# Summing the squares of a block norm on GpSimd before two ones-matmuls, in place of eight ones-matmuls

## The chip, the cores and the metric

One Trainium2 chip, all 8 NeuronCores. Every core runs the same program on its own share of the requests (1536 tokens) and reads the same weights; nothing is exchanged between cores. The metric is the device time of the slowest core in microseconds (us), as the median of several runs. The engines are named as in the profile: PE is TensorE (matmul), PEld its weight loads, DVE is VectorE, ACT is ScalarE, POOL is GpSimd, SP is SyncE.

## The reference

Two layers of a trunk. Every sub-layer takes its input through an RMS norm with a shift and a scale, and its result is added to the residual stream through a gate. Cut to what matters:

```python
def rms_norm(x, g):
    x32 = x.astype(jnp.float32)
    y = x32 * lax.rsqrt(jnp.mean(x32 * x32, axis=-1, keepdims=True) + EPS)
    return (y * g.astype(jnp.float32)).astype(x.dtype)
...
for i in range(DEPTH):          # DEPTH = 2, D_MODEL = 1024
    h = rms_norm(x, norm_mix_g[i]) * (1 + csc1) + csh1
    y = pool + latent attention (i even)  or  chunk_gmlp (i odd)   # then out projection
    x = x + cg1 * y
    h = rms_norm(x, norm_ffn_g[i]) * (1 + csc2) + csh2
    x = x + cg2 * swiglu(h, ffn_wg[i], ffn_wu[i], ffn_wd[i])
```

The mean in `rms_norm` runs over the 1024 channels of a token. This is the sum that the change rebuilds.

## The kernel before

The residual stream lives in SBUF as three blocks `xb[0..2]` of 512 tokens. Channels lie on the partitions: a block is 8 chunks of 128 partitions x 512 tokens, fp32. A sum over the channels of a token is therefore a sum over 8 chunks and over 128 partitions. The kernel takes it with matmuls against a matrix of ones (`ones`), which add over the partitions and write the same sum on all of them.

A norm of one block is: eight squares in bf16 (`xsq`, a ring of four tiles), eight ones-matmuls that accumulate into PSUM bank 7, then Ln and Exp on ACT (`rstd`, tile `xrs`), then for each chunk a product on DVE (`xtmp`, a ring of three tiles) and a shift into `hb` in bf16, on ACT for six chunks and on DVE for chunks 3 and 7 (`apply`, line 565).

The first three norms, at the start of the program, are written out in line (`Norm.stats`, line 554, and `apply`). The other nine come from the generator `Norm.gen` (line 577), and `stage` (line 611) weaves them into the matmul work of three transitions. They are named here by transition and block:

- A0, A1, A2: from the output projection of the attention layer into the first FFN;
- B0, B1, B2: from that FFN's last down-projection into the gating MLP (`gmlp`);
- C0, C1, C2: from the gating MLP's output projection into the second FFN.

Within a norm the squares are called s0 to s7, after their chunks.

`stage` takes one step of the main work, for example one output tile of 8 matmuls. It adds the number that the step yields to a debt (1.7 for a projection tile of 8 matmuls, 2.1 for a down-projection tile of 10, 3.4 for an FFN up pair of 16). Then it emits pieces of the oldest waiting norm until the numbers that these yield have paid the debt. A norm joins the queue when the last tile of its block has been emitted. Nothing else sets the order: each engine works through its own instructions in the order in which the program emits them, and waits where an instruction needs another engine's result. A wait of an instruction holds up all that follows on its engine.

In `gen` before, s0, s1, s3, s4, s6 and s7 are on ACT, s2 and s5 on DVE, and the ones-matmul of a chunk is emitted three squares later. The yields of one norm add up to 14.8.

GpSimd issues the weight DMAs: `Stream.done` frees a slot and at once issues the next weight load on the POOL queue, which waits there until PE has read the slot for the last time. Between the steps of the transitions stand four such issues after each output projection (the slots `wo` or `go`). After the first FFN come five issues for the `wd` slots and one for `wsT`. After the last `v_half` of the gating MLP come eight, for the slots `gu` and `gv` (lines 776 to 778). In the gating MLP POOL also multiplies two tiles in each `sp_tile` (line 752); the last two of these calls, `sp_tile(10)` and `sp_tile(11)`, fall beside C0.

Of the kernel before, what the change touches and what calls it, by code (L numbers as in the profile page):

```python
# [8 lines left out]
F32 = mybir.dt.float32  # L9
BF16 = mybir.dt.bfloat16  # L10
AF = mybir.ActivationFunctionType
ALU = mybir.AluOpType
# [8 lines left out]
def _esize(dt):  # L21
    return 2 if dt == BF16 else 4

class Prog:
# [25 lines left out]
    def new(self, name, shape, dt, high=False):  # L50
        fsz = int(np.prod(shape[1:]))
        nbytes = (fsz * _esize(dt) + 31) // 32 * 32
        taken = sorted(self.live.values())
        gaps, at = [], 0
        for a0, a1 in taken + [(self.size, self.size)]:
            if a0 - at >= nbytes:
                gaps.append((at, a0))
            at = max(at, a1)
        assert gaps, (name, nbytes, self.size - sum(y - x for x, y in taken), sorted((v, k) for k, v in self.live.items()))
        addr = gaps[-1][1] - nbytes if high else gaps[0][0]  # L60
        self.uid += 1
        name = "%s_%d" % (name, self.uid)
        t = self.nc.alloc_sbuf_tensor_at(name, list(shape), dt, offset=self.base + addr)
        name = t.name
        rec = {"w": [], "r": []}
        for (a0, a1, evd) in self.freed:
            if a0 < addr + nbytes and addr < a1:
                for s, v in evd.items():
                    rec["w"].append((0, 128, 0, fsz, s, v))
        self.recs[name] = rec  # L70
        self.live[name] = (addr, addr + nbytes)
        return t

    def drop(self, *tiles):
        for t in tiles:
            a0, a1 = self.live.pop(t.name)
            rec = self.recs.pop(t.name)
            evd = {}
            for x in rec["w"] + rec["r"]:
                if x[5] > evd.get(x[4], 0):  # L80
                    evd[x[4]] = x[5]
            self.freed.append((a0, a1, evd))
# [275 lines left out]
def build():  # L358
# [42 lines left out]
    with ExitStack() as es:  # L401
        P = Prog(nc, es)
        P.psum_banks(es)
        P.arena(es, 207 * 1024)
        new, drop = P.new, P.drop

        xb = [new("xb%d" % b, [128, 8, 512], F32) for b in range(3)]
        vecs = new("vecs", [128, NV], F32)
        ones = new("ones", [128, 128], BF16)
# [60 lines left out]
        def rstd(out, in_, n_, np_=128):  # L470
            P.act(out, in_, AF.Ln, bias=epsc[0:np_, EPSI[n_]:EPSI[n_] + 1])
            P.act(out, out, AF.Exp, scale=-0.5)
# [72 lines left out]
        class Norm:  # L545
            def __init__(self):
                self.sq = Ring([new("xsq%d" % i, [128, 512], BF16) for i in range(4)])
                self.rs = [new("xrs%d" % i, [128, 512], F32) for i in range(3)]
                self.tmp = Ring([new("xtmp%d" % i, [128, 512], F32) for i in range(3)])

            def close(self):
                drop(*self.sq.t, *self.rs, *self.tmp.t)

            def stats(self, b):
                ps = P.bank()
# [21 lines left out]
            def gen(self, l, w, b, hb):  # L577

                ps = P.banks[7]
                sqs = []  # L580

                def add(kc):
                    P.mm(ps[:], ones[:], sqs[kc][:], start=(kc == 0), stop=(kc == 7))

                yield 1.0
                for kc in range(8):
                    sq = self.sq.next()
                    sqs.append(sq)
                    if kc % 3 != 2:
                        P.act(sq[:], xb[b][:, kc, :], AF.Square)  # L590
                    else:
                        P.tt("dve", sq[:], xb[b][:, kc, :], xb[b][:, kc, :], ALU.mult)
                    if kc >= 3:
                        add(kc - 3)
                    yield 0.6
                for kc in range(5, 8):
                    add(kc)
                    yield 0.2
                rstd(self.rs[b][:], ps[:], 1024)
                yield 1.2  # L600
                for kc in range(8):
                    self.apply(l, w, b, hb, [kc])
                    yield 0.9
# [98 lines left out]
        def gmlp(need):  # L702
# [7 lines left out]
            P.dma("sp", bsbc[:], bsbc_d, "gmb")  # L710
            P.dma("sp", gvbc[:], gvbc_d, "gmg")
            vr = Ring([new("vraw%d" % i, [128, 1024], BF16) for i in range(3)])
            sqv = Ring([new("sqv%d" % i, [128, 512], BF16) for i in range(3)])
            tb = Ring([new("gtb%d" % i, [128, 512], F32) for i in range(3)])
            vts = {}

# [492 lines left out]
        W.more([new("wslotx%d" % i, [128, 2048], BF16) for i in range(8, 8)])  # L1209
        stage(ffn(0, need(0, 1)), fill, norms, 1, 0, hbs)  # L1210
        stage(gmlp(need(1, 0)), fill, norms, 1, 1, hbs)
        stage(ffn(1, need(1, 1)), fill, norms, None, None, hbs)

# [133 lines left out]
```

How the kernel before makes its waits and increments, by code:

```python
    def op(self, e, fn, reads, writes, inc=True):  # L181
        rr = [x for x in (self.reg(a) for a in reads) if x is not None]
        wr = [x for x in (self.reg(a) for a in writes) if x is not None]
        waits = self._waits(e, self._deps(rr, wr, e))
        eng = self.E[e]
        attach = (e != "pe")
        for s, v in (waits[:-1] if attach else waits):
            eng.wait_ge(self.sem[s], v)
        ins = fn(eng)
        if waits and attach:
            ins._wait_ge(self.sem[waits[-1][0]], waits[-1][1])
        if inc:
            ins.then_inc(self.sem["c_" + e], 1)
            self.cnt[e] += 1
            ev = ("c_" + e, self.cnt[e])
        else:
            ev = ("c_" + e, self.cnt[e] + 1)
        self._record(rr, wr, ev)
        self.nins += 1
        return ins
# [1 line left out]
    def dma(self, q, out, in_, key, slow=False):  # L202
        rr = [x for x in (self.reg(in_),) if x is not None]
        wr = [x for x in (self.reg(out),) if x is not None]
        waits = self._waits(q, self._deps(rr, wr))
        eng = self.E[q]
        for s, v in waits:
            eng.wait_ge(self.sem[s], v)
        k = self.dsem(key)
        side = out if wr else in_
        nm = side.tensor.name
        last = self.dlast.get(k)
        if last is not None and last != nm and self.known[q].get(k, 0) < self.dtot[k]:
            eng.wait_ge(self.sem[k], self.dtot[k])
            self.known[q][k] = self.dtot[k]
        self.dlast[k] = nm
        if slow:
```

## Time and profile before

| | |
|---|---|
| median of 3 runs | 1267.45 us (1266.27 to 1267.82) |
| profiled execution, its own time | 1267.72 us |
| span of its slowest core (core 2) | 1266.7 us; the eight cores 1261.2 to 1266.7 us |
| busy, share of the span | PE 90%, DVE 42%, ACT 32%, POOL 13% |
| mean granted TensorE clock of core 2 | 0.953 |

The span runs from the first to the last instruction of a core; the profiled execution's own time is 1.0 us longer than that. Busy shares are averages over stages with different limits, and a busy PE is not PE at its peak: matmuls overlap, so the time from one start to the next, not the duration of one, is what a matmul costs. The granted clock is 1.00 when TensorE has its full 2.4 GHz and 0.50 at 1.2 GHz.

### The profile page before, as it was taken

What the parts mean: (1) busy time and instruction counts of PE and PEld (TensorE: products, weight loads), DVE (VectorE), ACT (ScalarE), POOL (GpSimd) and SP (SyncE); (2) the same over time, 40 slices, a digit from 0 to 9 for tenths busy, and PEclk for the clock granted to TensorE, in tenths of its full rate; (3) what the DMA queues carried; (4) which work ended last, traced back from release to release, by engine and by line L of the source; (5) the groups of instructions that cost most, each with busy time, mean ns of one, the idle gap of its engine ahead of it and who ended that gap; (6) DMA issues with size and microseconds to landing.
All of it is one profiled execution on the core that took longest, in us unless ns stands there. A gap on an engine that the chain in (4) does not pass through costs nothing.

```text
span 1266.7 us, 17760 instructions; the slowest of 8 cores (1261.2 to 1266.7 us)
## 1 busy us (share of the span) xinstructions
PE 1141.6 (90%) x6857; PEld 552.1 (44%) x6857; DVE 526.9 (42%) x912; ACT 399.4 (32%) x619; POOL 165.2 (13%) x295
## 2 busy tenths in 40 slices
PE   2288767888879899999999999999999999999998
PEld 0133454555544344444444444444444444444443
DVE  2444686436216531133243256457841115225133
ACT  2244226666773621100100135553551110110100
POOL 1200235425120001000000001133100000000000
PEclk9988879778699999999999999999999999999999
DMA  9950405684996406322312403200913411400013
GB/s 220 200 89 1 82 9 93 118 138 85 168 157 114 67 1 100 65 36 51 66 34 50 84 1 69 40 1 2 168 32 60 74 34 34 84 17 1 1 72 128
DMA packets 25106, 90.04 MB, mean 71 GB/s; under 512 B 3392, under 2 KB 4032, under 8 KB 24256
## 3 DMA queue, kind: packets, MB, share of 16 engines
q0 software_dynamic: 20864, 72.90, 34.6%
q1 hardware_dynamic: 4160, 16.00, 3.8%
q8 instruction: 58, 0.95, 0.3%
q14 instruction: 24, 0.20, 0.1%
HBM read 153.85 MB, written 6.88 MB: 127 GB/s over the span
## 4 chain that ended last, share of the span: by engine, by line
PE 79%; DVE 7%; DMA 6%; ACT 3%; issue 2%; POOL 2%; SPq 0%; DVEq 0%; ACTq 0%; POOLq 0%
PE pb L230 77%; DMA xb<-x_in 3%; DMA wslot<-ada_w 2%; ACT pt L247 2%; PE pb L228 2%; DVE kT L274 1%; DVE xtmp L268 1%; DVE hy L259 1%; PE pb L239 1%; POOL qs L251 1%; DVE qf L274 1%; DVE pbf L259 1%; DVE ss L1007 0%; DVE qt L251 0%; DVE ytk L251 0%
## 5 line engine op out<-in xcount | busy, mean ns | idle before, releaser
L230 PE MATMUL pb<-hb,wslotx 128*128 128x512 bf16 x1440 | 319.9, 379 | 0.0
L251 DVE TENSOR_TENSOR apart<-pb,sg 128x512 bf16<-128x512 f32 x132 | 91.3, 692 | 357.3 <-PE pb L230 339.4
L247 ACT ACTIVATE sg<-pb 128x512 f32<-128x512 f32 x132 | 78.6, 597 | 471.1 <-PE pb L230 471.1
L230 PEld LDWEIGHTS pb<-hb,wslotx 128*128 128x128 bf16 x1440 | 140.8, 98 | 170.0
L268 DVE SCALAR_TENSOR_TENSOR xb<-pb,mod,xb 128x512 f32<-128x512 f32 x192 | 143.9, 750 | 132.7 <-PE pb L230 132.6
L230 PE MATMUL pb<-hb,wslot 128*128 128x512 bf16 x864 | 196.4, 383 | 0.0
L230 PE MATMUL pb<-apart,wslot 128*128 128x512 bf16 x768 | 167.1, 379 | 0.0
L247 ACT ACTIVATE pt<-pb,rk 128x1024 bf16<-128x1024 f32 (+1 forms) x128 | 118.7, 952 | 64.3 <-PE pb L230 62.8
L230 PEld LDWEIGHTS pb<-hb,wslot 128*128 128x128 bf16 x864 | 85.3, 99 | 104.0 <-issue 4.5
L230 PEld LDWEIGHTS pb<-apart,wslot 128*128 128x128 bf16 x768 | 75.1, 98 | 90.2
L230 PE MATMUL pb<-hy,wslot 128*128 128x512 bf16 (+1 forms) x336 | 84.7, 406 | 9.9 <-ACT hy L247 9.5
L230 PE MATMUL pb<-qT,kT 96*128 96x512 bf16 (+1 forms) x224 | 80.2, 448 | 0.5 <-issue 0.5
L230 PE MATMUL pb<-xsq,ones 128*128 128x512 bf16 x96 | 31.8, 441 | 44.0 <-ACT xsq L247 28.8
L268 DVE SCALAR_TENSOR_TENSOR xtmp<-xb,AA,xrs 128x512 f32<-128x512 f32 x96 | 67.2, 745 | 5.5 <-ACT xrs L247 5.4
L228 PEld LDWEIGHTS pb<-V,pt 128*128 128x128 bf16 x768 | 39.5, 109 | 59.2 <-issue 53.2
L247 ACT ACTIVATE xsq<-xb 128x512 bf16<-128x512 f32 x66 | 38.5, 622 | 76.9 <-PE pb L230 34.4
L230 PE MATMUL pb<-apart,wslotx 128*128 128x512 bf16 x288 | 62.5, 379 | 0.0
L230 PEld LDWEIGHTS pb<-hy,wslot 128*128 128x128 bf16 (+1 forms) x336 | 34.1, 103 | 58.3 <-issue 25.4
L228 PE MATMUL pb<-V,pt 128*128 128x65 bf16 x768 | 47.0, 211 | 13.5 <-ACT pt L247 12.0
L247 ACT ACTIVATE hb<-xtmp,mod 128x512 bf16<-128x512 f32 x54 | 37.5, 721 | 39.3 <-DVE xtmp L268 39.3
L230 PE MATMUL pb<-wslotx,hb 128*128 128x512 bf16 x192 | 45.4, 379 | 0.0
L230 PE MATMUL pb<-uTb,wslot 128*128 128x512 bf16 x192 | 43.9, 379 | 0.0
(125 smaller groups left out, 879.8 us busy)
## 6 DMA issues: line engine op xcount, KB each, us to landing
wslot<-ada_w POOLq DMA_DIRECT2D x48, 512.0 KB, 9.2
wslot<-ffn_wd POOLq DMA_DIRECT2D x16, 512.0 KB, 7.4
wslotx<-ffn_wu POOLq DMA_DIRECT2D x14, 512.0 KB, 10.4
xb<-x_in SPq DMA_DIRECT2D x6, 1024.0 KB, 22.6
wslotx<-ffn_wg POOLq DMA_DIRECT2D x12, 512.0 KB, 18.0
y<-xb SPq DMA_DIRECT2D x12, 512.0 KB, 2.6
wslot<-ffn_wg POOLq DMA_DIRECT2D x10, 512.0 KB, 6.6
wslot<-ffn_wu POOLq DMA_DIRECT2D x8, 512.0 KB, 7.2
```

Source lines behind the costliest of these rows:

```text
L228: return self.op("pe", lambda g: g.matmul(out, lhsT, rhs, start=start, stop=stop, skip_group_check=True), [lhsT, rhs], [out], inc=inc)
L230: return self.op("pe", lambda g: g.matmul(out, lhsT, rhs, start=start, stop=stop), [lhsT, rhs], [out], inc=inc)
L239: return self.op("pe", lambda g: g.transpose(out, in_, ident), [in_, ident], [out])
L247: return self.op("act", lambda g: g.activation(out=out, in_=in_, func=func, bias=bias, scale=scale), reads, [out])
L251: return self.op(e, lambda g: g.tensor_tensor(out=out, in0=in0, in1=in1, op=op), [in0, in1], [out])
L259: return self.op(e, lambda g: g.tensor_scalar(out=out, in0=in0, scalar1=s1, scalar2=None, op0=op0), reads, [out])
L268: return self.op(e, lambda g: g.scalar_tensor_tensor(out=out, in0=in0, scalar=sc, in1=in1, op0=op0, op1=op1), reads, [out])
L274: return self.op(e, lambda g: g.tensor_copy(out=out, in_=in_), [in_], [out])
```

## The change

Only `Norm.gen` computes differently. Squares go to fp32 tiles (`xsf`, a new ring of four), all eight of them on ACT. For each half of four chunks POOL makes two adds in place (s0+s1, s2+s3) and a third that adds the two sums into a bf16 tile. PE then multiplies `ones` with two such tiles, and both of these matmuls are emitted after everything of the second half. The yields of one norm add up to 16.1. To make room, the ring `xtmp` goes from three tiles to two (also for the norms at the start) and the ring `sqv` of the gating MLP from three to two. `stats` stays as it is.

```diff
         class Norm:
             def __init__(self):
                 self.sq = Ring([new("xsq%d" % i, [128, 512], BF16) for i in range(4)])
+                self.sf = Ring([new("xsf%d" % i, [128, 512], F32) for i in range(4)])
                 self.rs = [new("xrs%d" % i, [128, 512], F32) for i in range(3)]
-                self.tmp = Ring([new("xtmp%d" % i, [128, 512], F32) for i in range(3)])
+                self.tmp = Ring([new("xtmp%d" % i, [128, 512], F32) for i in range(2)])
...
             def gen(self, l, w, b, hb):
 
                 ps = P.banks[7]
-                sqs = []
-
-                def add(kc):
-                    P.mm(ps[:], ones[:], sqs[kc][:], start=(kc == 0), stop=(kc == 7))
-
                 yield 1.0
-                for kc in range(8):
+
+                for q in range(2):
+                    sf = [self.sf.next() for _ in range(4)]
+                    for i in range(4):
+                        P.act(sf[i][:], xb[b][:, 4 * q + i, :], AF.Square)
+                        if i % 2 == 1:
+                            P.tt("pool", sf[i - 1][:], sf[i - 1][:], sf[i][:], ALU.add)
+                        yield 0.65
                     sq = self.sq.next()
-                    sqs.append(sq)
-                    if kc % 3 != 2:
-                        P.act(sq[:], xb[b][:, kc, :], AF.Square)
-                    else:
-                        P.tt("dve", sq[:], xb[b][:, kc, :], xb[b][:, kc, :], ALU.mult)
-                    if kc >= 3:
-                        add(kc - 3)
-                    yield 0.6
-                for kc in range(5, 8):
-                    add(kc)
-                    yield 0.2
+                    P.tt("pool", sq[:], sf[0][:], sf[2][:], ALU.add)
+                    if q == 1:
+                        yield 0.6
+                        P.mm(ps[:], ones[:], first[:], start=True, stop=False)
+                        yield 0.6
+                        P.mm(ps[:], ones[:], sq[:], start=False, stop=True)
+                    first = sq
+                yield 0.3
                 rstd(self.rs[b][:], ps[:], 1024)
                 yield 1.2
                 for kc in range(8):
...
-            sqv = Ring([new("sqv%d" % i, [128, 512], BF16) for i in range(3)])
+            sqv = Ring([new("sqv%d" % i, [128, 512], BF16) for i in range(2)])
```

## Rows read from the trace of the kernel before

**Rows 1.** Page, part 4: the chain that ended last, share by engine.

```profile
PE 79%; DVE 7%; DMA 6%; ACT 3%; issue 2%; POOL 2%; SPq 0%; DVEq 0%; ACTq 0%; POOLq 0%
```

**Rows 2.** That chain in order of time: start us, us, what.

```profile
434.84 303.42 PE pb L230 x1405
```

**Rows 3.** Groups by line, PE, 376.5 to 945 us: busy us, mean ns, idle before.

```profile
L230 PE MATMUL pb<-xsq,ones 128*128 128x512 bf16 x72 | 20.6, 381 | 11.3 <-ACT xsq L247 5.7 <-DVE xsq L251 5.6
```

**Rows 4.** Timeline, PE: start us, us, what, count, idle before and its releaser.

```profile
376.51 15.70 PE L230 MATMUL pb<-hy,wslot 128*128 128x512 bf16 x72
...
421.41 3.62 PE L230 MATMUL pb<-hb,wslot 128*128 128x512 bf16 x16
427.78 0.38 PE L230 MATMUL pb<-xsq,ones 128*128 128x512 bf16 x1 [2.76 <-ACT xsq L247]
428.00 5.30 PE L230 MATMUL pb<-hb,wslot 128*128 128x512 bf16 x16
...
718.65 19.59 PE L230 MATMUL pb<-apart,wslot 128*128 128x512 bf16 x90
...
880.03 0.61 PE L230 MATMUL pb<-wsT,vraw 128*128 128x128 bf16 x8
...
886.48 0.59 PE L230 MATMUL pb<-xsq,ones 128*128 128x512 bf16 x2 [1.95 <-DVE xsq L251]
...
920.36 0.58 PE L230 MATMUL pb<-xsq,ones 128*128 128x512 bf16 x1 [2.62 <-ACT xsq L247]
```

**Rows 5.** Windows: us, busy of PE, PEld, DVE, ACT, POOL; clock; DMA.

```profile
428.70:429.70 1.00, 1.00 (x4) 0.41 (x3) 0.00 (x0) 0.00 (x0) 0.00 (x0) 0.50 0.00 0
...
886.40:890.00 3.60, 3.52 (x23) 1.96 (x24) 3.11 (x5) 1.15 (x2) 3.48 (x6) 1.00 0.98 160
```

**Rows 6.** Instructions of single tiles, DVE: count, ns min/median/max, first and last start us.

```profile
L251 DVE TENSOR_TENSOR xsq<-xb x30: 676/683/693, 8.9 to 926.4; 128x512 bf16<-128x512 f32 x30
...
L259 DVE TENSOR_SCALAR hy<-xtmp,mod x6: 486/486/2045, 56.6 to 120.7; 128x512 bf16<-128x512 f32 x6
```

**Rows 7.** Timeline, ACT, transitions A and B.

```profile
408.00 2.37 ACT L247 ACTIVATE xsq<-xb 128x512 bf16<-128x512 f32 x4
...
425.23 1.28 ACT L247 ACT_TABLE_LOAD   x1
...
755.36 1.65 ACT L247 ACTIVATE xsq<-xb 128x512 bf16<-128x512 f32 x3
```

**Rows 8.** Groups by line, POOL, whole span: its adds' nearest kin.

```profile
L251 POOL TENSOR_TENSOR uTb<-gtb,uTb 128x512 bf16<-128x512 f32 x24 | 27.2, 1153 | 77.5 <-DVE gtb L251 77.4
```

**Rows 9.** Timeline, POOL, start of the program.

```profile
57.10 1.28 POOL L251 TENSOR_TENSOR ropeq<-ropeq,gqr 128x512 f32<-128x512 f32 x1
```

**Rows 10.** Start of the program: timeline of DVE, of ACT, then of PE.

```profile
53.85 2.74 DVE L268 SCALAR_TENSOR_TENSOR xtmp<-xb,AA,xrs 128x512 f32<-128x512 f32 x4
...
54.64 2.05 ACT L247 ACTIVATE hy<-xtmp,mod 128x512 bf16<-128x512 f32 x3 [9.30 <-DVE xtmp L268]
...
88.65 2.24 PE L230 MATMUL pb<-hy,wslot 128*128 128x512 bf16 x4 [4.35 <-ACT hy L247]
```

**Rows 11.** Timeline, DVE, first FFN and end of the gating MLP.

```profile
440.12 2.07 DVE L268 SCALAR_TENSOR_TENSOR xtmp<-xb,AA,xrs 128x512 f32<-128x512 f32 x3
...
883.59 1.49 DVE L268 SCALAR_TENSOR_TENSOR vraw<-vraw,rsv,gvbc 128x1024 bf16<-128x1024 bf16 x1 [0.69 <-ACT rsv L247]
```

**Rows 12.** Timeline, POOL, where weight DMAs are issued in transitions B and C.

```profile
777.86 1.06 POOL L220 DMA_DIRECT2D wslot<-gm_w_out  x2 [57.96 <-PE pb L230]
...
781.14 0.54 POOL L220 DMA_DIRECT2D wsT<-wsT  x1
...
881.73 2.27 POOL L251 TENSOR_TENSOR uTb<-gtb,uTb 128x512 bf16<-128x512 f32 x2 [5.08 <-DVE gtb L251]
883.94 0.59 POOL L220 DMA_DIRECT2D wslotx<-ffn_wu  x1
...
887.64 0.59 POOL L220 DMA_DIRECT2D wslotx<-ffn_wg  x1
```

More of the change, by code:

```diff
@@ L547, in __init__ @@
                 self.sq = Ring([new("xsq%d" % i, [128, 512], BF16) for i in range(4)])
+                self.sf = Ring([new("xsf%d" % i, [128, 512], F32) for i in range(4)])
                 self.rs = [new("xrs%d" % i, [128, 512], F32) for i in range(3)]
-                self.tmp = Ring([new("xtmp%d" % i, [128, 512], F32) for i in range(3)])
+                self.tmp = Ring([new("xtmp%d" % i, [128, 512], F32) for i in range(2)])
             def close(self):
-                drop(*self.sq.t, *self.rs, *self.tmp.t)
+                drop(*self.sq.t, *self.sf.t, *self.rs, *self.tmp.t)
             def stats(self, b):
```

## The prediction

> **What bounds the kernel now.** I read the page's chain first: 79% of the span hangs on PE [rows 1]. The chain in order of time says how: after 434.84 us it is one unbroken run of 1405 matmuls in 303.42 us, 0.216 us each [rows 2]. So in the FFN and gating stages, with the nine woven norms between them, a matmul that goes saves 0.216 us, and a wait that PE meets costs its whole length. Next the groups of PE in that stretch: the 72 ones-matmuls of the nine norms had 11.3 us of idle time before them, put there by squares on ACT and DVE that came late [rows 3]. Then the timeline of PE for where: 2.76 us at A2, 1.95 at C0, 2.62 at C2 are the large ones [rows 4]. Last the granted clock around them. After the 2.76 us stall it was 0.50, the lower level of 1.2 GHz; after the 1.95 us stall it stayed at 1.00 [rows 5]. The spell costs: 16 matmuls took 5.30 us behind the stall, and 3.62 us just before it, 1.7 us more [rows 4]. C2's stall, nearly as long [rows 4], I count the same. So the norms now cost PE 11.3 us of waits and two clock spells of 1.7 us: 14.7 us beside the matmuls themselves.
>
> **What goes.** Six of eight ones-matmuls in nine norms: 54 x 0.216 = 11.7 us of PE. The 14.7 us of waits and spells go too, as far as nothing replaces them. The two DVE squares of each norm, 0.68 us each [rows 6], lie beside PE's run and bring nothing of their own.
>
> **What comes: the chain to the last sum.** An fp32 square I cost like the bf16 one, 0.59 us (four in 2.37) [rows 7]. An add of 128x512 on POOL isn't in the trace; the nearest is the product that reads an fp32 and a bf16 tile, 1.153 us [rows 8], then an all-fp32 one of 1.28 us [rows 9], and far below DVE's own 0.683 us for the same shape [rows 6]. I take 1.15: same engine, same size. One half of a norm then costs two squares (1.19), three adds one after the other (3.45), and three hand-overs between instructions that wait on each other, under 0.1 us each (the first shift starts about 0.1 us behind its product [rows 10]), 0.2 together: 4.85 us. The third and fourth square hide behind the first add. The second half can't overlap the first: `xsf` has four tiles, s4 writes the tile that the first half's last add still reads, so ACT waits there for POOL. From the start of s0 to a sum that PE can take: 2 x 4.85 = 9.7 us. Before, PE needed only the square of three chunks earlier.
>
> The Trainium skill (GPSIMD Engine Reference, Engine selection) says to leave elementwise work to VectorE, GpSimd being about twice as slow with two inputs. By twice DVE's 0.683 an add would be an estimated 1.37 us, the chain 1.3 us longer, and the sum below about 9 us higher (1299); no row of POOL is that slow, the widest being 1.28 [rows 9].
>
> **Against when PE arrives.** Both matmuls stand in PE's queue with the main work behind them, so a late sum stops everything. Following `stage` through the new yields gives the position of each.
>
> A0: s0 to s7 run on ACT while the projection tiles of their own block land, and the matmuls come after the fourth tile of the next block; the sum is ready about 3 us early. B0 likewise, about 2.5 us. No wait.
>
> A1: its squares stand on ACT behind the shifts of A0 and start at 408.5 (408.00 before [rows 7]; A0's shifts come a tile later and through two `xtmp` tiles). Its matmuls follow the fifth tile of block 2, 171 matmuls after 376.51 [rows 4]: 376.5 + 36.9 = 413.4. The sum is there at 408.5 + 9.7 = 418.2. PE waits 4.8 us. C1 has the same order: 4.8.
>
> A2: PE resumes at 418.2, runs three tiles and an up pair (40 matmuls, the first eight at half clock) to about 428.7. ACT still has the shifts of A1, a table load of 1.28 us [rows 7] for Silu, three products of 2.07 us [rows 11] with their shifts, and the second Silu: s0 starts near 434.9. The first matmul stands behind the third pair (435.5), its sum comes at 434.9 + 4.85 = 439.7: wait 4.2. The second finds its sum, since the fourth pair covers the other half. C2 the same.
>
> B1: s0 near 753.5 (755.36 before [rows 7], some two less: six ones-matmuls and B0's waits are gone, the shifts come a tile later). PE is there 193 matmuls after 718.65 [rows 4], at 760.3; the sum at 763.2: wait 2.9.
>
> B2: s0 at 774.0, the first add until 776.4. Then POOL's own queue comes in: five weight issues and `wsT` stand before the next add, from 777.86 to 781.68 before [rows 12], 3.8 us. The first half's sum comes at 782.6, PE asks after three u tiles at 779.4: 3.2. The second half then takes to 788.0 (u copies stand between the squares on ACT); PE, at half clock, asks near 786.1: 1.9. Together 5.1.
>
> C0: PE reaches `sp_tile(11)` 16 matmuls after 880.5 [rows 4], at 883.9, and waits 1.2 for `vraw`, done at 885.08 [rows 11]; the ones-matmuls hid that before. On POOL two multiplies (2.27) and eight weight issues (883.94 to 888.2 [rows 12]) stand between the first and the second add. So the first half is summed at 890.7, the second (with the two multiplies of `sp_tile(11)` in its way) at 897.7. PE asks after two more tiles, at 889.1: waits 1.6 and 6.8. Together 9.6.
>
> Sum: 4.8 x 2 + 4.2 x 2 + 2.9 + 5.1 + 9.6 = 35.6 us of waits. Nearly all are as long as the two that had a spell behind them, so I count one of 1.7 for each of the seven norms: 11.9.
>
> **What moves besides.** `xtmp` with two tiles: at the start DVE makes a product every 0.68 us and ACT a shift in about as much [rows 10]; the third product now waits for the first shift, about 0.25 us twice in each of three norms, and PE does wait for these (4.35 us at 88.65 [rows 10]): +1.5 us. Nothing if DVE's own stops cover it, 3 at most. `sqv` with two tiles: nothing, its reader is done long before the second next square; without that cover a reduction of some 0.7 us would sit in the 24 halves of v, which PE's seven PSUM banks still hide. Weight loads issued behind an add come up to 8 us later, for pairs that PE reaches over 15 us afterwards: nothing. Other addresses in SBUF: nothing known, +-1.
>
> **The sum against the profiled execution.** 1267.7 - 11.7 - 14.7 + 35.6 + 11.9 + 1.5 = 1290.3 us. This execution lies 0.3 us above the median of the runs, so the median to expect is 1290, slower by 1.8%.
>
> **Rivals.** *The cover holds (faster).* If every sum were ready when PE asks, only the removals and the start would count: 1267.7 - 11.7 - 14.7 + 1.5 = 1243. A0 and B0 do show such cover. It decides at the length of an add: the new terms shrink by some 42 x the shortening (six adds in seven late norms), so the balance tips where an add takes about 0.6 us, below DVE's 0.683 [rows 6]. Between that and 1.15 lies every smaller loss.
>
> *The clock stays up.* If the new stalls brought no spell, 11.9 falls out: 1278. For it: behind the 1.95 us at C0 the clock stayed up [rows 4, 5]. Against: behind A2's 2.76 us it fell, and each late norm has a wait that is longer.
>
> *The two engines get in each other's way.* A shift on DVE that takes 0.486 us took 2.045 [rows 6], starting at 56.6 and ending just after POOL's all-fp32 product of 57.10 to 58.38 [rows 9]. With adds of 1.28 the chain is 0.8 us longer at seven places, 5.5 us: 1296. With the two DVE shifts of a norm held for 1.5 us each ahead of A1, B1 and C1 as well, up to 1304. The Trainium skill (GPSIMD Engine Reference, Key points) names such contention, for DVE instructions in a two-port mode or with two SBUF inputs. Against it here: the adds of a norm begin when the shifts of the one before are all but done.
>
> *No change.* Adds near the balance point, or main work that gives the stalls back: nothing in the rows has slack behind PE.
>
> **How the numbers follow.** Forecast 0.60 (1284 to 1294), clock stays up 0.14 (1274 to 1283), engines collide 0.14 (1295 to 1304), cover holds 0.08, no change 0.04. Within 0.2% (2.5 us) is what a measurement of this kernel can't tell from no change. The range leaves the last two out below and a remainder above: 1270 to 1304. Faster 0.08, same 0.04, slower 0.88.
>
> **What would show it.** In the profile after: 18 woven ones-matmuls beside the 24 at the start; POOL adds of about 1.15 us, 54 of them; the ones-matmuls waiting for POOL some 35 us in all, longest at C0 and none at A0 and B0; granted clock 0.50 in spells behind A1, A2, B2, C0, C1, C2; ACT waiting for POOL before s4; the weight issues between the adds at B2 and C0. Wrong it would be with adds well under 1 us, with s0 of A1 several us earlier, or with stalls that leave the clock alone.

## The result, and the profile after

| | before | after |
|---|---|---|
| median of 6 runs each, on one chip | 1267.63 us | 1305.64 us |
| ratio, 95% interval | | 1.0306 [1.0285, 1.0328] |
| profiled execution: slowest core's span | 1266.7 us | 1303.7 us |

The ratios, and the times given with the experiments, leave out runs in which one die was disturbed. The change costs 38 us. The forecast was slower, with 1290; the measured time lies 1.6 us outside its range.

The page of the kernel after, its header, its busy line and part 4 (the chain by engine), which answers to [rows 1]:

```profile
span 1303.7 us, 17736 instructions; the slowest of 8 cores (1293.4 to 1303.7 us)
PE 1138.1 (87%) x6803; PEld 546.7 (42%) x6803; DVE 517.8 (40%) x894; ACT 409.1 (31%) x637; POOL 232.8 (18%) x349
PE 71%; DVE 8%; ACT 7%; POOL 5%; DMA 4%; issue 4%; SPq 0%; DVEq 0%; POOLq 0%; ACTq 0%
```

PE's share of the chain fell from 79% to 71%, and POOL's rose from 2% to 5%: some 65 us of the span now hang on GpSimd, where it was 25. The groups of PE between 370 and 985 us, the nine woven norms, say which waits these are; the last numbers are the idle time before the group and what ended it (the one of before is in [rows 3]):

```profile
L230 PE MATMUL pb<-xsq,ones 128*128 128x512 bf16 x18 | 7.9, 459 | 43.6 <-POOL xsq L251 43.6
L230 PE MATMUL pb<-wsT,vraw 128*128 128x128 bf16 x96 | 7.3, 219 | 1.3 <-DVE vraw L268 1.3
```

Eighteen matmuls are left of 72, and PE stands 43.6 us in front of them, where it stood 11.3 in front of the 72. With the 1.3 us at `vraw`, which the old order hid, the waits are 44.9 us; the prediction had 35.6. The timeline of PE shows each (start us, us, what, count, idle before and its releaser). The lines with `xsq` are, from the top, A0 (both matmuls), A1 (two lines), A2 (two), B0 (both matmuls), B1 (its second), B2 (two), C0 (two), C1 (its second) and C2 (two); the `vraw` line belongs to C0:

```profile
399.51 0.59 PE L230 MATMUL pb<-xsq,ones 128*128 128x512 bf16 x2
...
415.86 0.38 PE L230 MATMUL pb<-xsq,ones 128*128 128x512 bf16 x1 [0.22 <-POOL xsq L251]
420.91 0.59 PE L230 MATMUL pb<-xsq,ones 128*128 128x512 bf16 x1 [4.67 <-POOL xsq L251]
...
436.80 1.89 PE L230 MATMUL pb<-hb,wslotx 128*128 128x512 bf16 x8
442.57 0.59 PE L230 MATMUL pb<-xsq,ones 128*128 128x512 bf16 x1 [3.89 <-POOL xsq L251]
448.04 0.59 PE L230 MATMUL pb<-xsq,ones 128*128 128x512 bf16 x1 [4.87 <-POOL xsq L251]
...
753.66 0.59 PE L230 MATMUL pb<-xsq,ones 128*128 128x512 bf16 x2
...
774.80 0.38 PE L230 MATMUL pb<-xsq,ones 128*128 128x512 bf16 x1 [3.07 <-POOL xsq L251]
...
793.97 0.59 PE L230 MATMUL pb<-xsq,ones 128*128 128x512 bf16 x1 [2.82 <-POOL xsq L251]
...
799.43 0.38 PE L230 MATMUL pb<-xsq,ones 128*128 128x512 bf16 x1 [2.00 <-POOL xsq L251]
...
901.01 0.64 PE L230 MATMUL pb<-wsT,vraw 128*128 128x128 bf16 x8 [1.34 <-DVE vraw L268]
...
906.78 0.38 PE L230 MATMUL pb<-xsq,ones 128*128 128x512 bf16 x1 [1.68 <-POOL xsq L251]
914.08 0.58 PE L230 MATMUL pb<-xsq,ones 128*128 128x512 bf16 x1 [6.93 <-POOL xsq L251]
...
937.53 0.58 PE L230 MATMUL pb<-xsq,ones 128*128 128x512 bf16 x1 [4.58 <-POOL xsq L251]
...
960.15 0.38 PE L230 MATMUL pb<-xsq,ones 128*128 128x512 bf16 x1 [3.75 <-POOL xsq L251]
965.62 0.59 PE L230 MATMUL pb<-xsq,ones 128*128 128x512 bf16 x1 [5.09 <-POOL xsq L251]
```

| | A0 | A1 | A2 | B0 | B1 | B2 | C0 | C1 | C2 | sum |
|---|---|---|---|---|---|---|---|---|---|---|
| predicted wait, us | 0 | 4.8 | 4.2 | 0 | 2.9 | 5.1 | 9.6 | 4.8 | 4.2 | 35.6 |
| measured | 0 | 4.9 | 8.8 | 0 | 3.1 | 4.8 | 10.0 | 4.6 | 8.8 | 44.9 |

Seven of nine agree within 0.4 us. A2 and C2 have twice the wait: between 442.57 and 448.04 PE does nothing but one ones-matmul and then waits for the second half. The prediction had the fourth up pair standing there.

Clock, in windows behind each wait (us, busy of PE, PEld, DVE, ACT, POOL, granted clock, DMA share, GB/s), in the order A1, A2, B1, B2 first, B2 second, C0, C1, C2:

```profile
421.20:428.20 7.00, 7.00 (x26) 2.83 (x25) 2.97 (x5) 2.16 (x4) 1.14 (x3) 0.75 0.80 136
...
448.00:455.00 7.00, 6.96 (x24) 2.90 (x25) 0.69 (x1) 2.87 (x4) 0.00 (x0) 0.71 0.00 0
...
774.80:786.00 11.20, 11.20 (x52) 5.14 (x53) 8.50 (x13) 6.01 (x10) 0.00 (x0) 1.00 0.00 0
...
794.00:797.40 3.40, 3.40 (x9) 1.15 (x9) 0.00 (x0) 2.90 (x6) 1.94 (x2) 0.59 1.09 158
799.40:806.00 6.60, 6.57 (x23) 2.71 (x24) 4.07 (x7) 4.45 (x7) 0.00 (x0) 0.74 1.05 179
...
914.00:922.00 8.00, 7.92 (x25) 3.02 (x26) 3.39 (x5) 2.71 (x4) 0.00 (x0) 0.65 1.05 161
937.50:945.90 8.40, 8.37 (x26) 3.27 (x27) 2.96 (x5) 2.15 (x4) 1.48 (x3) 0.64 0.74 123
965.60:972.50 6.90, 6.88 (x21) 2.70 (x22) 0.38 (x1) 2.79 (x4) 0.00 (x0) 0.62 0.01 2
```

PE is busy all but throughout each window, so a window's length times what its clock lacks of 1.00 is what the spell cost: 7.0 x 0.25 = 1.75 at A1, 2.0 at A2, none at B1, 1.4 and 1.7 at B2, 2.8 at C0, 3.0 at C1, 2.6 at C2. Together 15.3 us; the prediction had seven spells of 1.7, 11.9.

These are one core's spells. In both kernels the waits are the same on all eight cores to some tenths of a us, but the clock does not answer to them alike. In the kernel before, behind the 2.76 us at A2 and the 2.6 at C2, it fell on five of the eight cores and stayed at 1.00 on three; on core 1, one of the three, 16 matmuls behind the wait take 3.61 us, where core 2 took 5.30 [rows 4]:

```profile
429.63 0.38 PE L230 MATMUL pb<-xsq,ones 128*128 128x512 bf16 x1 [2.76 <-ACT xsq L247]
429.84 3.61 PE L230 MATMUL pb<-hb,wslot 128*128 128x512 bf16 x16
```

In the kernel after, B1's wait is followed by a spell of 1.7 us on three cores and by none on the other five. Summed over windows of half a microsecond (PE's busy time times what the clock lacks of 1.00), the spells of the nine norms are 2.1 us before and 14.5 after, as the mean of eight cores.

**The books.** Start times of a single execution differ between cores by some us, so from here on a kernel's woven part is measured as "the stretch": the time from a core's first output-projection matmul (the start of transition A) to that core's end, as the mean of eight cores of the profiled execution. It was 889.4 us before and is 924.4 after: +35.0. With the terms as the mean of eight cores too, -11.7 (matmuls) -11.3 (old waits) -2.1 (old spells) +44.8 (new waits) +14.5 (new spells) = +34.2. Half of the 0.8 us between the two is a spell at the very start of transition A, which four cores have after and two before; the other half I can't place. The remaining 3 us of the 38 are not seen ahead of the stretch in these two executions: that part took 374.8 us before and 373.5 after, as the mean of the cores. But the slowest core, which the time is taken from, ended 2.6 us above the mean of the eight before, and 5.8 after.

### The profile page after: what moved, and what is told of

The parts are those of the page before. It is cut to its first block, busy times and chain, and to the rows that moved or that the text cites. A ratio compares the mean times of both kernels' runs of the same rounds, so it can differ in the third digit from the quotient of the medians.

```text
span 1303.7 us, 17736 instructions; the slowest of 8 cores (1293.4 to 1303.7 us)
## 1 busy us (share of the span) xinstructions
PE 1138.1 (87%) x6803; PEld 546.7 (42%) x6803; DVE 517.8 (40%) x894; ACT 409.1 (31%) x637; POOL 232.8 (18%) x349
## 4 chain that ended last, share of the span: by engine, by line
PE 71%; DVE 8%; ACT 7%; POOL 5%; DMA 4%; issue 4%; SPq 0%; DVEq 0%; POOLq 0%; ACTq 0%
PE pb L230 69%; DMA xb<-x_in 3%; ACT pt L247 3%; POOL xsf L251 3%; DVE xtmp L268 2%; PE pb L228 2%; DVE kT L274 2%; POOL xsq L251 1%; DMA wslot<-ada_w 1%; ACT xsf L247 1%; ACT hy L247 1%; PE pb L239 1%; DVE pbf L259 1%; ACT hb L247 0%; DVE qf L274 0%
## 5 line engine op out<-in xcount | busy, mean ns | idle before, releaser
L230 PE MATMUL pb<-hb,wslotx 128*128 128x512 bf16 x1440 | 323.5, 382 | 0.0
L230 PE MATMUL pb<-hy,wslot 128*128 128x512 bf16 (+1 forms) x336 | 87.7, 419 | 10.3 <-ACT hy L247 10.0
L230 PE MATMUL pb<-xsq,ones 128*128 128x512 bf16 x42 | 19.1, 551 | 77.4 <-POOL xsq L251 43.6
L268 DVE SCALAR_TENSOR_TENSOR xtmp<-xb,AA,xrs 128x512 f32<-128x512 f32 x96 | 70.6, 768 | 18.5 <-ACT xrs L247 14.7
L230 PE MATMUL pb<-qT,kT 96*128 96x512 bf16 (+1 forms) x224 | 76.8, 430 | 0.5 <-issue 0.5
L251 POOL TENSOR_TENSOR xsf<-xsf,xsf 128x512 f32<-128x512 f32 x36 | 45.2, 1269 | 113.6 <-ACT xsf L247 113.6
L247 ACT ACTIVATE xsf<-xb 128x512 f32<-128x512 f32 x72 | 41.1, 622 | 54.2 <-POOL xsq L251 27.9
L230 PE MATMUL pb<-uTb,wslot 128*128 128x512 bf16 x192 | 48.7, 412 | 0.0
```

Source lines behind the costliest of these rows:

```text
L230: return self.op("pe", lambda g: g.matmul(out, lhsT, rhs, start=start, stop=stop), [lhsT, rhs], [out], inc=inc)
L247: return self.op("act", lambda g: g.activation(out=out, in_=in_, func=func, bias=bias, scale=scale), reads, [out])
L251: return self.op(e, lambda g: g.tensor_tensor(out=out, in0=in0, in1=in1, op=op), [in0, in1], [out])
L268: return self.op(e, lambda g: g.scalar_tensor_tensor(out=out, in0=in0, scalar=sc, in1=in1, op0=op0, op1=op1), reads, [out])
```

## The experiments

My theory was that PE waits for sums that are late because the chain of squares and adds is about 10 us long and is emitted where PE arrives sooner; that the matmuls removed are worth their 0.216 us each; and that A2 and C2 doubled through the place of their two matmuls in the order. The rivals are named with each. All ratios are against the kernel before on the same chip.

**The debt carried from one stage to the next.** Each call of `stage` starts its debt at zero. I had carried the 0.6 that the projection stage had overpaid into the FFN stage; with zero one more piece fits behind each pair, and the second ones-matmul lands ahead of the fourth pair. In this kernel the debt is carried, as I had reckoned.

```diff
+        owed = [0.0]
...
         def stage(main, fill, norms, l, w, hbs):
-            debt = 0.0
+            debt = owed[0]
...
                 if not fill:
                     debt = 0.0
+            owed[0] = debt
```

> The changed kernel, with one thing more: a stage hands its unpaid debt or credit to the next stage instead of starting it at zero. Theory: the prediction went wrong at A2 and C2, because it carried the credit of 0.6 over from the projection stage and so put the fourth up pair between the two ones-matmuls; in the kernel they stand side by side and both halves of the chain are waited for (3.9 + 4.9 us at A2). With the credit carried, the pair stands between them, the second wait falls to under 1 us at A2 and C2, and the time falls by 8 to 11 us against the changed kernel, to about 1.023 of before. Rival: the excess is the longer adds alone (1.27 for 1.15 us, on a chain that the order doesn't change); then the sum of the waits is only spread otherwise and the time stays within 2 us of the changed kernel (1.030).

Measured: 1294.36 us, 1.0212 [1.0193, 1.0231]; ones-matmuls wait 33.6 us for POOL. A2 in PE's timeline:

```profile
444.36 0.58 PE L230 MATMUL pb<-xsq,ones 128*128 128x512 bf16 x1 [3.89 <-POOL xsq L251]
444.74 3.05 PE L230 MATMUL pb<-hb,wslot 128*128 128x512 bf16 x8
447.62 1.89 PE L230 MATMUL pb<-hb,wslotx 128*128 128x512 bf16 x8
449.35 0.38 PE L230 MATMUL pb<-xsq,ones 128*128 128x512 bf16 x1
```

The fourth pair stands between the two matmuls, and the second finds its sum; C2 looks the same. The wait saved is 43.6 - 33.6 = 10.0 us and the stretch 10.1 us shorter. The misplaced matmul is what made A2 and C2 double.

**The rings alone.** The kernel before, with the rings of the change (four fp32 tiles, two `xtmp`, two `sqv`) and nothing else of it.

```diff
+                self.sf = Ring([new("xsf%d" % i, [128, 512], F32) for i in range(4)])
...
-                self.tmp = Ring([new("xtmp%d" % i, [128, 512], F32) for i in range(3)])
+                self.tmp = Ring([new("xtmp%d" % i, [128, 512], F32) for i in range(2)])
...
-            sqv = Ring([new("sqv%d" % i, [128, 512], BF16) for i in range(3)])
+            sqv = Ring([new("sqv%d" % i, [128, 512], BF16) for i in range(2)])
```

> The kernel before, with only the rings of the change: two xtmp tiles for three, two sqv tiles for three, and the fp32 ring allocated and not used. Theory: the products at the start wait for the shifts, +1.5 us (0 to 3), ratio 1.001; the waits of the woven norms stay at about 11 us. Rival: the smaller rings or the moved addresses cost the woven norms or attention several us, ratio 1.004 or more, and are part of what the prediction missed.

Measured: 1270.66 us, 1.0021 [1.0003, 1.0039], some 2.7 us by the ratio. The waits of the woven norms stay at 11.3 us and the stretch at +0.6, so it is the start that pays, as forecast, but more than the 1.5: the time ahead of the stretch is 376.8 us, where it was 374.8. The seven other experiments with two `xtmp` tiles at the start have 376.1 to 377.9 there, the three with three tiles 371.6 to 374.1; the profiled execution of the change itself, with 373.5, is the exception.

**The matmuls later.** The change, with the first of the two ones-matmuls emitted 5.9 units of debt later, between three and four projection tiles of PE's work.

```diff
                     if q == 1:
-                        yield 0.6
+                        yield 6.5
```

> The changed kernel with 6.5 instead of 0.6 yielded between the last add and the first ones-matmul, so that PE gets to them some 6 us of main work later; nothing else changes. Theory (only the arrival of PE against a chain of 10.3 us decides): the waits of A1, A2, B1, B2, C1, C2 fall to 1 us or less each, C0 keeps about 2 to 3 us and its 1.3 before the position mixer, the clock spells go, and what stays is the saving: 1267.6 - 11.7 - 14.7 + 1.5 + about 4 = 1247, ratio 0.98 to 0.99. Rival (POOL's adds cost by what they take from DVE and ACT, or norms that end later make the FFN wait): the waits move to the consumers of hb, and the time stays above before, ratio 1.00 to 1.02.

Measured: 1273.58 us, 1.0029 [1.0011, 1.0047]. With one number the loss falls from 3.1% to 0.3%, and the stretch is 33.3 us shorter than after. The theory's 0.98 to 0.99 is missed, and the ratio lies in the rival's range: 13.2 us of waits for POOL are left (at A1, A2, C0, C1, C2; none at B), and a new one stands in the gating MLP. The norm of B2 ends later there, and its shifts on ACT stand between the squares of the gating MLP's own reduction (`sqv`), which come late. PE's timeline there:

```profile
805.43 1.89 PE L230 MATMUL pb<-hb,wslotx 128*128 128x512 bf16 x7
812.69 1.01 PE L230 MATMUL pb<-wsT,vraw 128*128 128x128 bf16 x8 [5.37 <-ACT sqv L247]
```

At B, where the matmuls come late enough, the adds cost PE no wait; what costs is that PE asks early. But the place can't be put off alike for every transition.

**The adds on VectorE.** The same six adds on DVE in place of POOL.

```diff
-                            P.tt("pool", sf[i - 1][:], sf[i - 1][:], sf[i][:], ALU.add)
+                            P.tt("dve", sf[i - 1][:], sf[i - 1][:], sf[i][:], ALU.add)
...
-                    P.tt("pool", sq[:], sf[0][:], sf[2][:], ALU.add)
+                    P.tt("dve", sq[:], sf[0][:], sf[2][:], ALU.add)
```

> The changed kernel with all 54 adds on DVE instead of POOL, in the same places of the program. Theory: an add of about 0.7 us makes the chain about 7 us, and the weight issues and multiplies on POOL no longer stand between the adds at B2 and C0; waits of some 17 us stay in all, mostly at A2 and C2 where both halves are waited for, and the time is near that of before: ratio 0.998 to 1.008. Rival: the adds stand on DVE among residual updates, shifts and products, which delay them as much as POOL's length did, or delay the residuals that PE needs; ratio 1.015 or more.

Measured: 1287.04 us, 1.0148 [1.013, 1.0166], outside my range and at the rival's edge; 29.8 us of waits for DVE, at all nine norms, A0 and B0 too. DVE's timeline at A1:

```profile
417.12 1.40 DVE L268 SCALAR_TENSOR_TENSOR xb<-pb,mod,xb 128x512 f32<-128x512 f32 x2
418.44 0.68 DVE L251 TENSOR_TENSOR xsf<-xsf,xsf 128x512 f32<-128x512 f32 x1
419.04 0.75 DVE L268 SCALAR_TENSOR_TENSOR xb<-pb,mod,xb 128x512 f32<-128x512 f32 x1
419.70 0.68 DVE L251 TENSOR_TENSOR xsf<-xsf,xsf 128x512 f32<-128x512 f32 x1
420.42 0.69 DVE L251 TENSOR_TENSOR xsq<-xsf,xsf 128x512 bf16<-128x512 f32 x1
```

An add of 0.68 us in place of 1.27 brings only 18 us. A residual update of the main work stands between the first two adds, and the chain at A1, from s0 (416.68) to the second matmul (425.68), takes 9.0 us: 1.35 less than with POOL, where six adds shorter by 0.59 would have saved 3.5. My sum by duration alone, a tip near 0.6 us, had no queue in it; the engine with the faster add is the busier one.

**The second half's tiles in another order.** s4 waits for the add that reads the first half's sums. With the second half in tiles 1, 3, 0, 2, the tiles that the first two adds free come first, and ACT starts before the third add.

```diff
-                    sf = [self.sf.next() for _ in range(4)]
+                    sf = [self.sf.t[i] for i in ((0, 1, 2, 3), (1, 3, 0, 2))[q]]
```

> The changed kernel with the four fp32 tiles handed out in another order in the second half: s4 and s5 get the tiles of s1 and s3, which the first two adds have already read, so that ACT doesn't wait for the first half's last add. Theory: the chain is bound by POOL alone then, two squares and six adds one after the other, about 9.1 us instead of 10.35; each of the seven late norms waits some 1.2 us less, and the time falls by 7 to 10 us against the changed kernel, to 1.023 to 1.025 of before. Rival (POOL paces the chain anyway, the wait of ACT costs nothing): within 2 us of the changed kernel, 1.030.

Measured: 1293.61 us, 1.0164 [1.0101, 1.0227]; waits 33.1 us, stretch 12.7 us shorter than after, somewhat more than expected. The hand-over from POOL to ACT between the halves is part of the chain, as the prediction had it: from s0 to the second sum A1 now takes 9.15 us (412.61 to 421.76) where the change takes 10.35.

**The weight loads out of the way at C0.** The eight weight issues on POOL's queue, which stand between the first adds of C0, are emitted six tiles later.

```diff
-            for i in range(4):
-                W.done(("gu", i))
-                W.done(("gv", i // 2, i % 2))
             v_norm(11)
             yield next(outs)
             yield next(outs)
             sp_tile(11)
+            for _ in range(4):
+                yield next(outs)
+            for i in range(4):
+                W.done(("gu", i))
+                W.done(("gv", i // 2, i % 2))
```

> The changed kernel with the eight weight loads at the end of the gating MLP issued six tiles of the output projection later, behind the adds of C0 in POOL's queue instead of between its first and second. Theory: C0's sum comes about 4.3 us earlier, its two waits on POOL (1.7 and 6.9 us) shrink to some 4 in all, and the time falls by 4 to 6 us, to 1.026 of before; the later loads land in time. Rival (the sum of C0 waits for something else, or the weights come late for the FFN): the time stays at 1.030 or rises.

Measured: 1304.71 us, 1.0239 [1.0176, 1.0303] on a chip whose before was 1272.6; the interval is too wide to tell it from the change by time. In the traces waits fall from 43.6 to 40.4 us, the sum of C0 comes 9.79 us after `sp_tile(11)` in place of 13.07, and the stretch is 2.1 us shorter, where 4 to 6 were expected. The issues do hold the adds up there, by 3.3 us of the 4.3 they last: with them gone the second add still waits for the fourth square, and 5.5 us of waits are left at C0 where I had put some 4.

**Pairs only.** One add to each two squares, four ones-matmuls to a norm: a shorter chain, and four of the eight ones-matmuls removed.

```diff
+                sqs = []
+                for j in range(4):
+                    sf = [self.sf.next() for _ in range(2)]
+                    P.act(sf[0][:], xb[b][:, 2 * j, :], AF.Square)
+                    yield 0.65
+                    P.act(sf[1][:], xb[b][:, 2 * j + 1, :], AF.Square)
...
+                    P.tt("pool", sq[:], sf[0][:], sf[1][:], ALU.add)
+                    yield 0.65
+                yield 1.5
+                for j in range(4):
+                    P.mm(ps[:], ones[:], sqs[j][:], start=(j == 0), stop=(j == 3))
+                    if j == 2:
                         yield 0.6
```

> The changed kernel with only the first level of adds: POOL adds squares in pairs into four bf16 tiles (four adds for six), and four ones-matmuls are left of eight instead of two; 1.5 is yielded before them. The chain is two squares and four adds, about 6.3 us, and ACT doesn't wait for POOL. Theory (arrival against chain length): the waits on POOL fall from 44 us to about 10, most of them at C0 and A2, 36 matmuls fewer save 7.8 us, and the time is 0.995 to 1.004 of before. Rival (any add on POOL in the norm stops PE by about as much, whatever the length of the chain): 1.015 or more.

Measured: two runs, 1271.45 and 1270.19 us, beside 1272.6 for before, too few for an interval. Stretch 888.1 against 889.4, waits 11.3 us, as many as before. The 36 matmuls less (7.8 us) are nearly eaten: the spells grow from 2.1 to 6.2 us as the mean of eight cores, and the wait at `vraw`, 1.4 us, is open again.

**No adds.** The six adds of each norm are left out and the squares go to bf16 tiles, so a norm sums only chunks 3 and 7; order and the two matmuls stay.

```diff
-                            P.tt("pool", sf[i - 1][:], sf[i - 1][:], sf[i][:], ALU.add)
...
-                    P.tt("pool", sq[:], sf[0][:], sf[2][:], ALU.add)
```

> The changed kernel with the six adds of each woven norm left out: the squares are bf16 and the two ones-matmuls read those of chunks 3 and 7 alone, so six of eight squares don't enter the norm. Same order of the program otherwise. Theory (the cover holds once the adds are gone): no ones-matmul waits more than about 1 us except near the table loads of A2 and C2, no clock spell, and the time is 1267.6 - 11.7 - 14.7 + 2.7 + 2 to 6 = 1246 to 1250, ratio 0.983 to 0.986; the adds and what they bring then cost 55 to 60 us. Rival (ACT with all eight squares is late by itself): waits of 10 us or more stay, ratio above 0.99.

Measured: 1257.72 us, 0.9878 [0.9819, 0.9937]; stretch 876.0, 48 us under the change. So all of the loss, and more, comes with the adds and the fp32 squares they read. The interval by time would allow the 0.983 to 0.986 expected, but the stretch does not: it is 13.4 us shorter than before, where this asked for some 20 to 24. 7.7 us of waits are left, for ACT, mostly 3.47 at A2 and 3.33 at C2, where the squares stand behind Silu and its table load. In this order of the program the "cover holds" rival at 1243 could not have been reached even with adds that take no time.

**The emission alone, without the change.** If what counts is where PE asks, the kernel before should gain from that as well: all eight ones-matmuls stay, but are emitted behind all eight squares and a pause. No add, no POOL; eight bf16 square tiles (two `xtmp` in the woven norms and two `sqv` make room), the debt carried.

```diff
-                    if kc >= 3:
-                        add(kc - 3)
                     yield 0.6
-                for kc in range(5, 8):
-                    add(kc)
+                yield 2.0
+                for kc in range(8):
+                    P.mm(ps[:], ones[:], sqs[kc][:], start=(kc == 0), stop=(kc == 7))
                     yield 0.2
```

> The kernel before, without GpSimd: all eight ones-matmuls of a woven norm are kept but emitted behind all eight squares, 2.0 later, with eight bf16 square tiles (two xtmp tiles in the woven norms, two sqv tiles) and the credit carried from stage to stage. Theory (the waits in front of the ones-matmuls, not their number, are what can be had): the 11.3 us of waits and two clock spells of before mostly go, 10 to 13 us are saved with no matmul removed, ratio 0.990 to 0.993. Rival (the waits only move to the consumers of the norm): within 0.997 to 1.003.

Measured: 1254.69 us, 0.9882 [0.9859, 0.9906]; stretch 876.0. Groups of PE:

```profile
L230 PE MATMUL pb<-xsq,ones 128*128 128x512 bf16 x72 | 17.7, 379 | 0.0
```

No wait is left in front of 72 matmuls, and no core has a spell in the norms. The stretch is 13.4 us shorter than before. The old waits (11.3) and spells (2.1 as the mean of eight cores) come to as much. But 1.1 us of waiting at `vraw` is new, so 1.1 us of the gain has a source that I can't name. The place of the matmuls, the carried debt and the eight tiles were not tried apart.

**The best with pairs, and with the tree.** Both with the debt carried, the weight issues of C0 later, and three `xtmp` tiles at the start; the pairs with a pause of 3.5, the tree (the sums of the change, tiles in the order 1, 3, 0, 2) with a pause of 5.5, or 2.5 in transition B.

```diff
...
                     if q == 1:
-                        yield 0.6
+                        yield 2.5 if (l, w) == (1, 0) else 5.5
...
```

> Pairs on POOL (four adds, four ones-matmuls), 3.5 yielded before the matmuls, the credit carried, the eight weight loads issued behind C0's adds, and the norms at the start with three xtmp tiles again. Theory: the 11 us of waits that pairs still had at A2, B2, C0 and C2 fall below 4, and with 36 matmuls fewer the time is 0.984 to 0.990 of before. Rival (the later matmuls delay Ln and Exp, and with them the copies on ACT that the FFN and the gating MLP need): 0.994 or more.

> The whole two-level tree of the changed kernel, with what the single experiments showed: the other order of the fp32 tiles, 5.5 (2.5 in the transition into the gating MLP) yielded before the first ones-matmul, the credit carried, the weight loads behind C0's adds, three xtmp tiles at the start. Theory: waits on POOL of 3 to 8 us in place of 44, all 54 matmuls saved: 0.981 to 0.988 of before. Rival (a chain of 9 us can't be covered in these transitions): 0.993 or more.

Measured: pairs 1259.6 us, 0.9917 [0.99, 0.9934], a little above what was expected; 5.2 us of waits for POOL and 3.1 at the gating MLP's `sqv`. Tree: 1254.16 us, 0.9875 [0.9857, 0.9893], within what was expected, at its edge. Groups of PE with the tree:

```profile
L230 PE MATMUL pb<-xsq,ones 128*128 128x512 bf16 x18 | 6.3, 378 | 7.7 <-POOL xsq L251 7.7
```

The tree and the kernel before with late matmuls can't be told apart by time. The stretch differs by 2.2 us (873.8 and 876.0): the tree saves 11.7 us of matmuls and has 7.7 us of waits that the other has not.

All kernels together, by one floor: the late kernel of before waits for no ones-matmul (stretch 876.0), so a kernel with n woven ones-matmuls should take 876.0 - 0.216 x (72 - n) and its waits (those at the ones-matmuls and at `sqv`, on the slowest core). What is left over stands beside the clock spells of the norms, read as above, as the mean of eight cores:

| kernel | stretch, us | n | waits, us | left over, us | clock spells, us |
|---|---|---|---|---|---|
| before | 889.4 | 72 | 11.3 | 2.1 | 2.1 |
| after | 924.4 | 18 | 43.6 | 16.5 | 14.5 |
| debt carried | 914.3 | 18 | 33.6 | 16.4 | 14.5 |
| adds on DVE | 906.2 | 18 | 29.8 | 12.1 | 9.8 |
| other tile order | 911.7 | 18 | 33.1 | 14.3 | 12.0 |
| weight loads later | 922.3 | 18 | 40.4 | 17.6 | 15.6 |
| matmuls later | 891.1 | 18 | 18.6 | 8.2 | 6.5 |
| pairs | 888.1 | 36 | 11.3 | 8.6 | 6.2 |
| no adds | 876.0 | 18 | 7.7 | 4.0 | 3.5 |
| pairs, late | 879.5 | 36 | 8.3 | 3.0 | 1.7 |
| tree, late | 873.8 | 18 | 7.7 | 1.8 | 0.4 |

So each kernel comes out of its matmuls, its waits and its clock spells to within 2.4 us. The spells, not the length of the waits alone, make the remainder: the pairs wait as long as the kernel before and have three times its spells.

## Why the prediction was off

The direction and the mechanism were right: sums late, PE at the head of its queue, longest at C0, none at A0 and B0. The step that failed is **"The second finds its sum, since the fourth pair covers the other half. C2 the same."** I had followed the order of emission with a debt carried over between stages; each stage starts at zero, and the fourth pair came after both matmuls. That is 4.87 us at A2 and 5.09 at C2 by the timeline, and the first experiment gave back 10.1 us of the stretch when the debt was carried. Added to the forecast it makes 1300. With the other waits 0.7 us shorter than forecast in all, and the spells of the slowest core 3.4 longer, it is 1303.

Step by step, the rest:

- *The matmuls, -11.7.* Held to within 2 us: between the two late kernels, 54 matmuls less and 7.7 us of waits more give 4.0 us, and 2.2 were found.
- *Old waits and spells, -14.7.* The two spells were read on one core, and three of the eight have none behind the same waits: 13.4 as the mean of the cores, and 13.4 by the late kernel of before.
- *An add at 1.15 us.* It took 1.27, as POOL's groups show (the product beside them is that of [rows 8]):

```profile
L251 POOL TENSOR_TENSOR xsf<-xsf,xsf 128x512 f32<-128x512 f32 x36 | 45.2, 1269 | 113.6 <-ACT xsf L247 113.6
L251 POOL TENSOR_TENSOR uTb<-gtb,uTb 128x512 bf16<-128x512 f32 x24 | 27.2, 1155 | 70.2 <-DVE gtb L251 70.2
...
L251 POOL TENSOR_TENSOR xsq<-xsf,xsf 128x512 bf16<-128x512 f32 x18 | 22.7, 1262 | 1.5
```

 I had the all-fp32 row of 1.28 in [rows 9], of the same engine and size, and took the other one; the time goes with the type of the inputs, not with the operation or the type of the output. By twice DVE's time, the Trainium skill (GPSIMD Engine Reference, Engine selection) had the add at an estimated 1.37; the measured ratio is 1.27 / 0.683 = 1.86, so the trace agrees with its "about" and the truth lies between my value and its own.
- *The chain of 9.7 us.* At A1 it took 10.35, from s0 on ACT at 410.56 to the second matmul on PE at 420.91; ACT stands 2.91 us for POOL between the halves, as forecast:

```profile
410.56 2.18 ACT L247 ACTIVATE xsf<-xb 128x512 f32<-128x512 f32 x4
415.64 2.19 ACT L247 ACTIVATE xsf<-xb 128x512 f32<-128x512 f32 x4 [2.91 <-POOL xsq L251]
```

 The wait grew by 0.1 only. PE asked 5.1 us after s0, where I had 4.9, and 0.38 of what it then stood was filled by the first ones-matmul, which is not counted as waiting: that the wait at A1 agrees is in part luck. Against the start of A both s0 (1.3 us) and PE (1.5) came later than I had them. What moved both is a clock spell at the start of A, which this core has and core 0 has not (the first 4 us of A on core 7, then on core 0):

```profile
377.20:381.20 4.00, 4.00 (x15) 1.57 (x14) 1.61 (x8) 0.00 (x0) 0.00 (x0) 0.61 1.02 170
374.10:378.10 4.00, 4.00 (x19) 1.86 (x19) 2.50 (x9) 0.63 (x1) 0.00 (x0) 1.00 1.06 174
```

 On core 0, s0 and PE come 31.6 and 36.6 us after the start of A, where I had 32.0 and 36.9, and the wait is the same 4.9.
- *B2 and C0, the weight issues in POOL's queue.* 4.8 for 5.1 and 10.0 for 9.6. POOL's timeline at C0 shows eight issues of 0.54 to 0.60 us ahead of the second add:

```profile
902.90 0.58 POOL L220 DMA_DIRECT2D wslotx<-ffn_wu  x1
903.42 0.58 POOL L220 DMA_DIRECT2D wslotx<-ffn_wg  x1
903.97 1.33 POOL L251 TENSOR_TENSOR xsf<-xsf,xsf 128x512 f32<-128x512 f32 x1
905.38 1.26 POOL L251 TENSOR_TENSOR xsq<-xsf,xsf 128x512 bf16<-128x512 f32 x1
```

- *Clock spells, 11.9.* Mis-sized: 15.3 on the slowest core, 14.5 as the mean of eight. Their number on the slowest core was right by chance, seven: none at B1, two at B2. They are not all of one length: 1.4 to 3.0 us.
- *The start, +1.5.* 2.7 by the rings alone; the profiled execution of the change does not show it.

Of the rivals, *the clock stays up* is out at six of seven norms, and *the cover holds* is out even without adds. *The engines collide* would have given a time near the one measured (up to 1304). Its first part came true, adds near 1.28 us; its second did not: the 18 shifts on DVE, the instruction that had once taken 2.045 us, are all short. None of them ran during an add, so this case does not test what they do to each other.

```profile
L259 DVE TENSOR_SCALAR hb<-xtmp,mod x18: 485/486/489, 406.1 to 984.7; 128x512 bf16<-128x512 f32 x18
```

## What to carry to other kernels

Before work is taken off the busiest engine, ask when that engine asks for what replaces it: here 54 matmuls (11.7 us) were bought with a chain of 10 us on ACT and POOL, and the two matmuls that were left asked before its end. Each late sum cost its whole wait, and most a clock spell on top. Where side work is woven into an in-order queue, its position there can be worth more than its instructions: in this kernel the same eight matmuls emitted later, with the debt carried, gave 1.2%, as much as the whole tree gave with its own place put right. When an order is followed, follow it with the state that the emitter really has at each call; a counter reset that I overlooked was most of my error.

## What the hardware showed beside that

- A POOL add of two fp32 tiles of 128x512 takes 1.27 us, whether it writes fp32 or bf16; the product of an fp32 and a bf16 tile of that size takes 1.155.
- The length of a wait alone does not say whether TensorE's clock falls. The same wait of 2.76 us in the kernel before was followed by a spell at 0.50 (1.2 GHz) on five cores and by none on three, where the clock stayed at 1.00 (2.4 GHz). On the slowest core after, it stayed at 1.00 behind 3.07 us at B1, and fell behind 2.82 and 2.00 us at B2. Ahead of B1's wait PE had run for more than 40 us without a stop, but ahead of A1's, which has a spell, for 38; between B2's two waits it ran 3.4 us, partly at the low clock. No run here separates what makes the difference.
